# One channel group of a depthwise convolution: from four 64x64 blocks of the array to sixteen 32x32 blocks, with another way of adding the partial sums

## What is computed

```python
z = h @ w_in                       # q, k, v, ret_gate, conv_glu, gate_A, gate_B
# branch A: retention, 4 heads, then * silu(ret_gate), then @ w_ret_out
# branch B: GLU -> causal depthwise conv, width 31 -> LayerNorm -> silu -> @ w_conv_out
u = glu[..., :CONV_DIM] * jax.nn.sigmoid(glu[..., CONV_DIM:])
c = lax.conv_general_dilated(u_pad, conv_w[:, None, :], window_strides=(1,),
                             padding='VALID', feature_group_count=CONV_DIM)
c = jax.nn.silu(layer_norm(c + conv_b, conv_ln_g, conv_ln_b))
# merge of both branches @ w_out, LN1, then a mixture of 32 experts (top 1 of 4 groups,
# top 2 of 8 in it), the per-layer embedding, and LN2
```

## Time and profile before

| | |
|---|---|
| median of 3 runs | 926.77 us (925.39 to 926.88) |
| the profiled execution | 927.27 us, of which 925.1 us are the span of the instructions |
| TensorE busy | 860.6 us, 93% of the span |
| VectorE busy | 422.5 us, 46% |
| ScalarE busy | 263.5 us, 28% |
| read from HBM | 258.38 MB, and 13.09 MB written |

### The profile page before, as it was taken

The page is one execution under the profiler, slowest core; times in us unless marked ns, Lnnn a source line. Parts: engine busy times, 40 slices in busy tenths (PEclk is TensorE's granted clock), DMA queues, the critical chain, the costliest instruction groups (busy, mean ns, idle before and its releaser), DMA issues.

```text
span 925.1 us, 16495 instructions
## 1 busy us (share of the span) xinstructions
PE 860.6 (93%) x6604; PEld 554.6 (60%) x6604; DVE 422.5 (46%) x781; ACT 263.5 (28%) x362; POOL 49.4 (5%) x89
## 2 busy tenths in 40 slices
PE   8999999999999899899999998989888889898975
PEld 5997777889999796675444444434343434444431
DVE  5588999989967468864311110101010101011035
ACT  5454235454237533433111211112121211111110
POOL 1300000000000000000000000000000000000000
PEclk9999999999999999999999999999999999999997
DMA  8835233143342435737999999999999999999961
GB/s 316 274 143 147 91 137 137 46 139 135 137 151 97 176 137 226 320 137 292 405 421 422 422 422 422 422 423 421 423 421 422 423 422 422 422 423 421 421 240 57
DMA packets 40516, 266.66 MB, mean 288 GB/s; under 512 B 6214, under 2 KB 6486, under 8 KB 9632
## 3 DMA queue, kind: packets, MB, share of 16 engines
q1 hardware_dynamic: 36064, 255.30, 68.9%
q0 software_dynamic: 4416, 10.86, 3.6%
HBM read 258.38 MB, written 13.09 MB: 293 GB/s over the span
## 4 chain that ended last, share of the span: by engine, by line
PE 56%; DMA 32%; DVE 6%; ACT 3%; issue 2%; SPq 1%; DVEq 0%; ACTq 0%
DMA raw_x<-wstream 31%; PE ps L1584 12%; PE ps L1271 7%; PE ps L1273 6%; PE ps L1272 6%; PE ps L1595 3%; PE ps L1555 3%; PE ps L1308 2%; PE ps L1290 2%; PE ps L1310 2%; PE ps L1309 2%; ACT w_hi L472 1%; PE ps L1375 1%; DVE w_lo L722 1%; PE ps L1318 1%
## 5 line engine op out<-in xcount | busy, mean ns | idle before, releaser
L1584 PE MATMUL ps<-raw_x,xs 128*64 128x512 f32 x1024 | 233.6, 596 | 36.2 <-DMA raw_x<-wstream 35.0
L1584 PEld LDWEIGHTS ps<-raw_x,xs 128*64 128x64 f32 x1024 | 79.9, 136 | 161.2 <-issue 159.2
L1595 PE MATMUL ps<-raw_x,actT 128*64 128x512 f32 x512 | 117.8, 597 | 0.0
L722 DVE TENSOR_TENSOR w_lo<-raw_dense,w_hi 128x2048 fp32r<-128x2048 f32 x44 | 101.8, 2313 | 33.1 <-ACT w_hi L472 33.0
L1197 DVE COPY actT<-ps 128x256 f32<-128x256 f32 x32 | 13.6, 424 | 222.7 <-PE ps L1602 222.7
L855 DVE SCALAR_TENSOR_TENSOR cT_sb<-uT_sb,conv_par,cT_sb 128x350 f32<-128x350 f32 x210 | 106.5, 573 | 0.6
L472 ACT ACTIVATE w_hi<-raw_dense 128x2048 fp32r<-128x2048 f32 x44 | 84.0, 1908 | 79.6 <-PE ps L1290 44.6
L1271 PE MATMUL ps<-hT_hi,w_hi 128*128 128x320 f32 x304 | 95.5, 314 | 0.2 <-issue 0.2
L1273 PE MATMUL ps<-hT_hi,w_lo 128*128 128x320 f32 x304 | 93.9, 309 | 0.0
L1272 PE MATMUL ps<-hT_lo,w_hi 128*128 128x320 f32 x304 | 93.9, 309 | 0.0
L1203 DVE SCALAR_TENSOR_TENSOR act_rows<-gate_silu,slot_weight,ps 64x512 f32<-64x512 f32 x32 | 23.7, 740 | 140.2 <-ACT gate_silu L661 140.2
(11 more groups left out here) (290 smaller groups left out, 1055.2 us busy)
## 6 DMA issues: line engine op xcount, KB each, us to landing
raw_x<-wstream SPq DMA_DIRECT2D x192, 1024.0 KB, 24.2
raw_dense<-wstream SPq DMA_DIRECT2D x45, 1024.0 KB, 4.9
y_rows<-rows_sb POOLq DMA_DIRECT2D x10, 256.0 KB, 8.8
ln_gb<-ln POOLq DMA_DIRECT2D x2, 1024.0 KB, 5.6
y_gathered<-y_rows SPq DMA_DIRECT2D x4, 512.0 KB, 5.0
const<-consts SPq DMA_DIRECT2D x1, 1294.5 KB, 12.3
rows_sb<-x SPq DMA_DIRECT2D x2, 512.0 KB, 3.7
ln_gb<-ln_in POOLq DMA_DIRECT2D x1, 1024.0 KB, 5.0
```

Of the source, the lines that this page charges most:

```text
L722: tt(wlo[:, i % 2, :], raw_d[:, i % RAW_D, :], whi[:, i % 2, :].bitcast(F), ALU.subtract).then_inc(ss("lo_ready"), 1)
L1584: m = mm(ps[rows_at, 1, :], xs[:, 4 * half + k, :], w[i][:, k, :], start=half == 0 and k == 0, stop=half == 1 and k == 3)
L1595: m = mm(ps[64 * b:64 * b + 64, 4, :], aT[:, 2 * half + k, :], w[:, k, FF * b:FF * b + FF], start=half == 0 and k == 0, stop=half == 1 and ...
```

## The change

The 31 taps of group 0 are now cut into four 32x32 blocks each instead of two 64x64 blocks. Strip `i` (channels 32i to 32i+31) goes to bank `i`, and tap `k` puts it into partitions 32(k mod 4) and on. So the sixteen 32x32 blocks of the array all have work, and each strip's sum comes out in four parts, one in each quarter of its bank's partitions: banks 0 to 3 in place of 7 and 3.

The parts are summed in another way. ScalarE copies the four banks to `conv_parts` in SBUF, and a new function `conv_first_sum`, which stands on TensorE behind chunk 9, adds them: for each strip one product with a 128x32 matrix of four stacked identities (`C_EYE4`, 32 more columns of `const`), whose result goes to that strip's partitions of bank 7. ScalarE then copies the whole of it with the bias, behind `hi(11)`. VectorE's two additions are gone, and those who waited for `conv0_added` wait for `conv0_ready`.

```diff
+conv_parts = area("v", 4 * 4 * CCOLS).put("conv_parts", [128, 4, CCOLS], F)
...
             if i == 10:
                 act.wait_ge(ss("conv0_psum"), 1)
-                for at, bank in ((slice(0, 64), 7), (slice(64, 128), 3)):
-                    go(cT[at, 0, :], ps[at, bank, 0:CCOLS], ACT.Identity, bias=conv_par[at, 0, CONV_W:CONV_W + 1]).then_inc(ss("conv0_ready"), 1)
+                for n in range(4):
+                    go(conv_parts[:, n, :], ps[:, n, 0:CCOLS], ACT.Copy).then_inc(ss("conv0_parts_in"), 1)
+            if i == 11:
+                act.wait_ge(ss("conv0_folded"), 1)
+                go(cT[:, 0, :], ps[:, 7, 0:CCOLS], ACT.Identity, bias=conv_par[:, 0, CONV_W:CONV_W + 1]).then_inc(ss("conv0_ready"), 1)
...
-            if i == 10:
-                for at, other, bank, c in ((slice(0, 64), slice(64, 128), 7, 0), (slice(64, 128), slice(0, 64), 3, 1)):
-                    dve.wait_ge(ss("conv0_ready"), c + 1)
-                    tt(cT[at, 0, :], cT[at, 0, :], ps[other, bank, 0:CCOLS], ALU.add).then_inc(ss("conv0_added"), 1)
...
-            for k in range(0, CONV_W, 2):
-                for tap in (k, k + 1):
-                    if tap < CONV_W:
-                        pe.wait_ge(ss("diag_ready"), tap + 1)
-                        for i, bank in ((0, 7), (1, 3)):
-                            at = slice(64 * i, 64 * i + 64)
-                            j = (tap + i) % 2
-                            m = mm(ps[64 * j:64 * j + 64, bank, 0:CCOLS], tap_diag[tap][at, at], uT[at, 0, tap:tap + CCOLS],
-                                   start=tap < 2, stop=tap >= CONV_W - 2)
+            for tap in range(CONV_W):
+                pe.wait_ge(ss("diag_ready"), tap + 1)
+                c = slice(32 * (tap % 4), 32 * (tap % 4) + 32)
+                for i in range(4):
+                    at = slice(32 * i, 32 * i + 32)
+                    m = mm(ps[c, i, 0:CCOLS], tap_diag[tap][at, at], uT[at, 0, tap:tap + CCOLS], start=tap < 4, stop=tap >= CONV_W - 4)
             m.then_inc(ss("conv0_psum"), 1)
+
+        def conv_first_sum():
+
+            pe.wait_ge(ss("conv0_parts_in"), 4)
+            for i in range(4):
+                m = mm(ps[32 * i:32 * i + 32, 7, 0:CCOLS], const[:, C_EYE4:C_EYE4 + 32], conv_parts[:, i, :], start=True, stop=True)
+            m.then_inc(ss("conv0_folded"), 1)
...
-                if blk == 0 and half == 0:
-                    conv_first()
+                if blk == 0:
+                    (conv_first_sum if half else conv_first)()
```

More of the change, by code:

```diff
@@ L52 @@
 C_P = C_FOLD + 36
-C_N = C_P + 1
+C_EYE4 = C_P + 1
+C_N = C_EYE4 + 32
 NOWHERE = 4096
@@ L91, in _constants @@
     c[:, C_P] = p
+    c[:, C_EYE4:C_N] = np.tile(np.eye(32), (4, 1))
     return c.astype(np.float32)
@@ L263, in _program @@
         "heads_T heads_copied kz_ready q_scaled scores masked kv_ready kv_out state_new o_ready on_ready "
-        "diag_ready conv0_psum conv0_ready conv0_added taps_begun states_out ret_p_out out_tile route_hi route_lo "
+        "diag_ready conv0_psum conv0_parts_in conv0_folded conv0_ready taps_begun states_out ret_p_out out_tile route_hi route_lo "
         "onT_psum at_ready at_hi at_lo taps_done mean_ready centred squared var_ready cstd_ready conv_norm "
@@ L1401, in _ @@
         pe.wait_ge(ss("row_free"), 6 + 2 * TILES)
-        pe.wait_ge(ss("conv0_added"), 2)
+        pe.wait_ge(ss("conv0_ready"), 1)
         projected(3, 0, V_BANKS[1])
```

## The result

The changed kernel takes 928.5 us (median of 20 runs, 925.49 to 934.29), the kernel before 925.8 us beside it (20 runs, 922.49 to 927.46): a ratio of 1.0039, 95% interval 1.0025 to 1.0052. It is slower by 0.4%, where 0.2% of gain were forecast. The profiled execution shown here is the fastest of the 20 (span 923.4 us), so it is not its span but the stretch around the change that I compare.

The account below looks back on a forecast made before the run. TensorE bounds the kernel around the change, VectorE nearly so, expert-weight DMA late. TensorE would be ready 2.42 us sooner, but `lo(10)` caps the gain: 926.77 - 1.90 = 924.87 us, range 923.2 to 926.9 (forecast's own 924.1 to 925.6).

Parts of the forecast that it names:

- C: Length of the new convolution on TensorE: taken as 6.4 us, between 4.98 and 7.75.
- the 6.9 us: Longest convolution (6.91 us) for which the low part of chunk 10 still sets its start; a longer L1375 would refute the forecast.
- The upper end: Convolution length if instruction supply binds: 248 pairs at the experts' gather's 29.6 ns, plus 0.41 us, 7.75 us.
- the prediction's own sum: When TensorE is ready for chunk 10: 82.82 + 6.4 + 7.56 + 0.74 = 97.52 us, in place of 99.94.
- The strip products: Four products behind chunk 9 that add the strips' parts on TensorE: 0.74 us together.
- The copies: ScalarE's four copies of the banks ahead of the strip sums: 2.2 us, hidden under chunk 9's 7.56 us.
- The cap by `lo(10)`: Chunk 10 waits for VectorE's low part, ending at 97.92 us, which limits the gain to 1.90 us.
- Whether it lasts: After chunk 10 VectorE's rotation comes 2.11 us sooner, so the 1.90 us shift carries through to the end.
- Supply binds: Rival: convolution pairs come no faster than 29.6 ns, 7.75 us; 1.07 us gained, 925.70 us; chance 0.12.
- Fewer blocks at once: Rival: fewer than sixteen blocks work together in the convolution; eight give 9.56 us and 927.5, four 936.7; chance 0.10.
- The 36.6 us of strict order: Rival's variant: convolution matmuls run strictly in program order, 124 x 0.295 us, 954 us in all; chance 0.02.
- The clock: Rival: half-clock stretches, lost near chunk 10 (926.6 us, chance 0.04) or gained at 389.6 us (923.2 us, chance 0.08).

Follow-up runs that it names:

- three parts: Changed kernel with the convolution's taps spread as 80, 80 and 88 pairs inside chunk 8, at the old place and inside chunk 9: 923.99 us, ratio 0.9984.
- the hold: Changed kernel with SP's load of chunk 12 held back until the convolution is through: 923.43 us, ratio 0.9989 to the kernel before.
- the second run: Changed kernel without an edit, profiled once more: 926.84 us, one run.
- the extra load: Changed kernel with one more, unused load of 0.98 MB put by SP just ahead of chunk 12's load: 927.95 us, one run.
- the list shifted: Changed kernel with 20 tiny unused products (80 instructions) on TensorE ahead of chunk 8: 927.15 us, one run.
- two parts: Changed kernel with the convolution's taps split as 128 pairs inside chunk 8 and 120 at the old place: 924.40 us, ratio 0.9989.

## Why the prediction was wrong

**The step that failed is C**, the length of the new convolution, taken at 6.4 us between 4.98 and 7.75. It was 11.13 and 10.03 us in the two profiles of the changed kernel, outside both ends, and over the 6.9 us that the prediction had named as what would make it wrong. The upper end, "if the supply of instructions binds", had the right resource and the wrong form: I took supply as a steady pace, 29.6 ns a pair from the gather, and it is a stock that is refilled in blocks. Between the holes the pace is what I had hoped: with three parts 80 records last 2.46 us, of which the last is 0.45 itself (the median of a record's length), so (2.46 - 0.45) / 79 = 25.4 ns from start to start, and with the hold the convolution without its hole is 7.13 - 0.82 = 6.31 us, next to the 6.4 taken. The holes came on top, 2.97 + 0.66 + 0.28 + 0.86 = 4.8 us after the first 33 loads and their 0.19 us. With the measured C the prediction's own sum comes out: 82.82 + 11.13 + 7.56 + 0.74 = 102.25, chunk 10 later by 2.31 us, and 2.27 were measured; for the second run 1.21 and 1.17. No other term of this sum failed.

Why no row warned of it: the gather's row has 72 pairs in all, and the old convolution used a pair each 77 ns. No row that I had read of before has 128 pairs in a row at such a pace, and so none could show what happens then. The Trainium skill has the mechanism ("Runtime: NRT & Kernel Launch", "Instruction fetch mechanics"): the list comes in blocks of 16 KB, 256 instructions, by a DMA queue of the engine's own. The trace agrees, with packets of 16 KB on the queue of that kind. The Trainium skill calls the cost of passing a block's edge mostly hidden; in the old convolution no hole is seen in 9.56 us, in the new one the second hole was 2.17 and 2.97 us.

**The other terms held.** `lo(10)` is where it was forecast, 96.10 here, 22.53 us after chunk 8 began, and 97.92 - 75.38 = 22.54 in before. The strip products take 100.40 - 99.68 = 0.72 us (0.74 forecast). The copies take 1.53 us (2.2 forecast) under chunk 9. The cap by `lo(10)` was never reached in the changed kernel. Where it could have been, with the hold and with three parts, chunk 10 comes 22.85 and 22.95 us after chunk 8: a gain of 1.7 and 1.6 us. For the 7.13 us of the run with the hold, just over the 6.91 up to which the cap would bind, the prediction's sum gives 82.82 + 7.13 + 7.56 + 0.74 = 98.25, a gain of 1.69; 1.71 were measured. With `lo(10)` moved out of the way the second stayed at 22.95 and the first became 22.66, of which 0.18 are the convolution (6.95 in place of 7.13). So even there TensorE was last, with `lo(10)` within 0.3 us of it.

**Whether it lasts.** The shift goes through: with the hold the gain at chunk 13 is still 1.7 us (45.47 us after chunk 8 began, 47.18 in the kernel before), and the medians differ by 1.5, with an interval of the ratio that reaches 1. The medians of the changed kernel and the kernel before differ by 2.7 us, of which this stretch gives 1.2 to 2.3; the rest is not placed.

**The rivals.** "Supply binds" is the one that came, but with 10 to 11 us in place of 7.75, and so on the other side of no change. "Fewer blocks at once" gave the right sign and nearly the right time (9.56 us and 927.5 for eight blocks) by the wrong cause: a count of blocks would not change with a load on another queue, nor would its loss sit in two holes. The 36.6 us of strict order are not seen. "The clock" has a share: among the 20 executions of the changed kernel the six with a mean granted clock of 0.993 took 926.64 to 928.53 us, the five with 0.986 to 0.988 took 931.09 to 934.29. Why some have more half-clock stretches is not settled. Of the profiles only the one with the extra load has one inside the convolution, from the end of its long hole on; the two of the changed kernel have none there.

**What stays open.** That queue 8's packets are TensorE's own list is inferred from the holes that move with them; no view says whose list a packet holds. For it speaks the number of packets in the whole run: 25 in the kernel before, 26 in the changed one, which has 124 pairs more in TensorE's list, and 27 with the list shifted. The first hole, after 87 to 114 loads, has no packet of queue 8 beside it in the changed kernel's trace; with the hold it is still there and ends at 84.13, while a packet is on its way from 83.32 to 84.70, so not every hole is tied to a packet that the trace shows. Its cause stays open, and so does why the shifted list has none. Why chunk 12's load takes 8 us there, 8.2 in the kernel before as well, while it took 4.7 behind the convolution and 5.0 with three parts, was not tried.

## What to carry to other kernels

Cutting products into smaller blocks multiplies instructions, and the list of instructions is itself a stream from memory: count how many pairs of load and product stand together and how fast they are used, and look at which transfer is issued at the same moment. Here parts of 80 to 88 pairs ran without a hole, a part of 128 and the whole of 248 did not, though one of 120 did, so the length alone does not decide. The same taps gained 0.16% in three parts, just clear of the noise, and lost 0.4% in one. A wait that ends in `issue`, at a fixed place in the list and with a length that varies, asks for a shift of the list and a shift of the transfers, which told it here from the engine's own limits. When work is moved off a wait, look at the place where it lands as well: eight taps moved behind chunk 17 brought a wait of 2.89 us there.

## What the hardware showed that I had not expected

Sixteen 32x32 blocks take fp32 products from a single list at a mean of 25 ns a pair, some 73% of the blocks' own pace (0.295 / 16 = 18.4 ns, by the pass of 0.295 us behind the earlier trace rows). The first 32 weight loads of a part come at once, in 0.23 us as the row with two parts shows, some 7 ns each; the 33rd comes late, and 0.19 us of pause follow. This is alike in every run with 32x32 blocks, and not in the kernel before. A pause of TensorE of 2.52 us inside the convolution left its granted clock at 1.00 for the whole stretch from 81.00 to 92.10; with the extra load TensorE paused for 3.66 us, from 86.80 on, and the clock fell to 0.50, the lower of its two levels, at 90.1.
